# Moving the v products, transposes and mean squares of an mLSTM head within a hand-ordered schedule

## The reference

```python
p = jnp.exp(dmat - m_t[..., None]) * jnp.einsum('bhtd,bhsd->bhts', qc, kc)
num = w_inter[..., None] * jnp.einsum('bhtd,bhdv->bhtv', qc, C) + jnp.einsum('bhts,bhsv->bhtv', p, vc)
den = w_inter * jnp.einsum('bhtd,bhd->bht', qc, n) + jnp.sum(p, axis=-1)
h_c = num / jnp.maximum(jnp.abs(den), jnp.exp(-m_t))[..., None]
...
hs = rms_norm(hs) * h_norm.astype(f32).reshape(H, dv)
out = jax.nn.sigmoid(o.astype(f32)) * hs.reshape(B, S, H * dv)
return out.astype(h.dtype) @ w_out
```

## The kernel before

| half e | PE, after its 12 matmuls | ACT, after `w_hi` | DVE, after `w_lo` | POOL |
|---|---|---|---|---|
| 6 + 5h | scores(h), L1784 | | | |
| 7 + 5h | | exp(h) into `weights`, L870 | | mask(h), L587 |
| 8 + 5h | | | probs(h), L1241 | |
| 10 + 5h | products with v (h), L1766 to L1768 | | | |
| 11 + 5h | | squares, L878 and L881 | | |
| 12 + 5h | | tanh into `o_sig`, L862 | mean squares h_ms(h), L1250 | pow, L595; sigmoid, L597; then mask(h+1) |
| 13 + 5h | | | gated(h), L1260 | |
| 14 + 5h | transposes of gated(h), L1755 | | | |
| 15 + 5h | | o_hi(h), L888 | o_lo(h), L1274 | |

## Time and profile before

### The profile page before, as it was taken

One profiled execution on the slowest core, in us unless ns is written; L12 is line 12 of the kernel. 1 busy time (PEld: TensorE's weight loads), 2 busy tenths in 40 slices (PEclk: granted clock), 3 DMA queues, 4 the chain that ended last, 5 costly groups with the idle time before them and its releaser, 6 DMA issues.

```text
span 1179.1 us, 17187 instructions
## 1 busy us (share of the span) xinstructions
PE 1160.9 (98%) x5926; PEld 989.2 (84%) x5926; DVE 922.5 (78%) x1006; ACT 632.1 (54%) x920; POOL 165.2 (14%) x168
## 2 busy tenths in 40 slices
PE   5999999999999999999999999999999999999998
PEld 5888888888888888888888888888888888888887
DVE  6899997998889979888886547888885456777667
ACT  4444565666653556655554445555554455555442
POOL 1000140101221220221220001221220001221200
PEclk9999999999999999999999999999999999999999
DMA  9999999999999976987876577788775666666552
GB/s 367 397 401 402 400 355 341 360 406 372 337 362 362 400 206 179 266 232 231 246 235 215 194 231 223 210 260 235 213 249 180 206 185 185 197 188 179 202 176 86
DMA packets 260603, 314.57 MB, mean 267 GB/s; under 512 B 6241, under 2 KB 187177, under 8 KB 251849
## 3 DMA queue, kind: packets, MB, share of 16 engines
q1 hardware_dynamic: 259488, 312.50, 79.5%
q0 software_dynamic: 592, 1.22, 0.4%
q10 hardware_dynamic: 474, 0.21, 0.1%
HBM read 311.80 MB, written 2.11 MB: 266 GB/s over the span
## 4 chain that ended last, share of the span: by engine, by line
PE 73%; DMA 12%; DVE 8%; issue 3%; POOL 2%; ACT 1%; SPq 0%; DVEq 0%; ACTq 0%
PE ps L1484 27%; PE ps L1490 14%; PE ps L1524 9%; PE ps L1526 9%; PE ps L1525 9%; DMA m<-in_l_w_mod_dram 6%; DVE acc L1112 3%; DMA mod_raw<-in_l_w_mod_dram 3%; DMA raw<-in_l_w_in_dram 2%; DVE w_lo L1093 2%; POOL small L595 1%; PE ps L1593 1%; PE ps L1594 1%; DMA x<-in_x_dram 1%; PE ps L1652 1%
## 5 line engine op out<-in xcount | busy, mean ns | idle before, releaser
L662 ACT ACTIVATE w_hi<-raw 128x1024 fp32r<-128x1024 f32 x384 | 406.0, 1058 | 347.3 <-PE ps L1526 156.0
L1093 DVE TENSOR_TENSOR w_lo<-raw,w_hi 128x1024 fp32r<-128x1024 f32 x384 | 471.3, 1230 | 151.8 <-ACT w_hi L662 150.5
L1484 PE MATMUL ps<-hm,w_hi 128*128 128x512 f32 x1406 | 338.8, 391 | 0.2 <-DVE hm L1381 0.2
L1484 PEld LDWEIGHTS ps<-hm,w_hi 128*128 128x128 f32 x1406 | 257.2, 188 | 49.2 <-DVE hm L1381 0.4
L1490 PEld LDWEIGHTS ps<-hm,w_lo 128*128 128x128 f32 x1408 | 182.7, 191 | 8.2
L1490 PE MATMUL ps<-hm,w_lo 128*128 128x256 f32 x1408 | 185.2, 283 | 0.0
L1593 PE MATMUL ps<-w_hi,hm 128*128 128x512 f32 x380 | 150.8, 397 | 0.0
L1594 PE MATMUL ps<-w_lo,hm 128*128 128x512 f32 x380 | 148.0, 390 | 0.0
L1596 PE MATMUL ps<-w_hi,hm 128*128 128x512 f32 x352 | 137.2, 390 | 0.0
L1526 PE MATMUL ps<-w_hi,act_lo 128*128 128x512 f32 x344 | 133.8, 389 | 0.0
L1525 PE MATMUL ps<-w_lo,act_hi 128*128 128x512 f32 x344 | 133.8, 389 | 0.0
(11 more groups left out here) (204 smaller groups left out, 1140.4 us busy)
## 6 DMA issues: line engine op xcount, KB each, us to landing
raw<-in_l_w_up_dram SPq DMA_DIRECT2D x88, 1024.0 KB, 5.8
raw<-in_l_w_in_dram SPq DMA_DIRECT2D x96, 512.0 KB, 12.1
mod_raw<-in_l_w_mod_dram SPq DMA_DIRECT2D x48, 1024.0 KB, 7.5
raw<-in_l_w_down_dram SPq DMA_DIRECT2D x44, 1024.0 KB, 5.0
m<-in_l_w_mod_dram SPq DMA_DIRECT2D x32, 640.0 KB, 14.2
raw<-in_l_w_out_dram SPq DMA_DIRECT2D x16, 1024.0 KB, 8.8
m<-in_l_w_mod_dram SPq DMA_DIRECT2D x15, 768.0 KB, 12.7
mod_third<-in_l_w_mod_dram SPq DMA_DIRECT2D x8, 1024.0 KB, 7.9
```

Source lines behind the costliest of these rows:

```text
L662: nc.scalar.activation(w_hi[:, v % 4, :], raw_half(v), ACT.Copy).then_inc(w_hi_made, 1)
L1093: nc.vector.tensor_tensor(w_lo[:, v % 4, :], raw_half(v), w_hi[:, v % 4, :].bitcast(f32), ALU.subtract)\
L1484: return mm(ps[:, 4 + w % 4, :], w_hi[:, v % 4, j * P:(j + 1) * P], both, start=(k == 0), stop=stop, skip_group_check=True)
```

## The change

E_PV goes from 10 to 11 and E_HT from 14 to 15; E_SCORES stays. All that hangs on these two offsets moves by one half: on PE the products with v of head h now stand in half 11 + 5h, the half of the next head's scores, and directly ahead of them in the order of `attend`; the transposes go to half 15 + 5h. On ACT the squares go to half 12 + 5h (behind the next head's exponentials), tanh to 13 + 5h, o_hi to 16 + 5h. On DVE the mean squares go to 13 + 5h, gated to 14 + 5h, o_lo to 16 + 5h. Half 13 + 5h is also that of the next head's probs, and in DVE's `attend` the block of the mean squares is moved ahead of the block of probs. POOL's order is not touched. No instruction is added or removed.

```diff
@@ -88,7 +88,7 @@
-    E_SCORES, E_PV, E_HT, E_HEAD = 6, 10, 14, 5
+    E_SCORES, E_PV, E_HT, E_HEAD = 6, 11, 15, 5
     E_GATE = 19
@@ -1233,14 +1233,6 @@
             def attend(e):
 
-                h = head_at(e, E_SCORES + 2)
-                if h is not None:
-                    dve.wait_ge(masked, h + 1)
-                    dve.wait_ge(scores_made, h + 1)
-                    wait_from_1(dve, pv_done, h)
-                    nc.vector.scalar_tensor_tensor(out=probs[:], in0=ps[:, 1, 0:SEQ + P],
-                                                   scalar=float(DK) ** -0.5, in1=weights[:],
-                                                   op0=ALU.mult, op1=ALU.mult).then_inc(probs_made, 1)
                 h = head_at(e, E_PV + 2)
                 if h is not None:
                     dve.wait_ge(den_sq_made, h + 1)
@@ -1251,6 +1243,14 @@
                                                        scalar=a_em[:, 2 + t, h:h + 1],
                                                        in1=h_ss[:, t:t + 1], op0=ALU.max, op1=ALU.add)\
                                  .then_inc(h_ms_made, 1)
+                h = head_at(e, E_SCORES + 2)
+                if h is not None:
+                    dve.wait_ge(masked, h + 1)
+                    dve.wait_ge(scores_made, h + 1)
+                    wait_from_1(dve, pv_done, h)
+                    nc.vector.scalar_tensor_tensor(out=probs[:], in0=ps[:, 1, 0:SEQ + P],
+                                                   scalar=float(DK) ** -0.5, in1=weights[:],
+                                                   op0=ALU.mult, op1=ALU.mult).then_inc(probs_made, 1)
```

## The result

The changed kernel takes 1186.87 us (median of 6, 1185.95 to 1187.57), the kernel before, run beside it, 1181.61 (median of 6, 1177.57 to 1181.84). The ratio is 1.0059, 95% interval 1.0047 to 1.0072: slower by about 0.6%. The forecast was 1187.0. Run again beside other executions of the kernel before (e9), the changed kernel gave 1185.90 and 1.0045 [1.0028, 1.0061]. The profiled execution has a span of 1185.1 us, against 1179.1 before, and a granted clock of 0.999.

The account below looks back on a forecast made before the run. DVE's queue, with its waits for the mask, was taken to pace the heads; after the change, a 17.97 us loop would. +5.7 us by half 41 and -0.4 in head 6 give +5.3 on 1181.7: 1187.0 us, range 1183.0 to 1193.2.

Parts of the forecast that it names:

- The pow: POOL's pow in heads 0 to 6 shortens from 1.60 to 0.72 us; rival that it stays 1.60, chance 0.15.
- Mean squares to probs: On DVE, from start to start, 2.14 us instead of 3.02, with `w_lo` (1.14 us) now paid in full ahead.
- The loop: Through all engines, transposes of one head to the next: 17.97 us, 17.37 without g_lo, setting the pitch.
- The wait for `w_hi`: DVE newly waits about 0.6 us per head for ACT's `w_hi`, because the loop exceeds DVE's own 17.14 us.
- the rival of DVE's queue alone: The loop doesn't bind; DVE's queue sets a pitch of 17.14 us: +1.8 us, 1183.5 us, chance 0.13.
- PE's wait for gated: In the heads, PE waits for gated about 1 us per head instead of 0.5; transposes 18.0 us apart.
- DVE is unmoved up to the `w_lo` of half 12: Starting point of the sum, at 249.06 us on DVE, from which head 0's transposes come at 258.28.
- my signs of being wrong: Gated less than 2.7 us later in head 0, or a wait for DMA data at `w_hi` or `add_mod`.
- The end of the stage: Head 5's transposes at 347.53, +5.7 us at half 41's scores, -0.4 us in head 6, in all +5.3 us.
- From span to time: 2.6 us between span and median, taking the forecast span of 1184.4 us to a time of 1187.0 us.
- The rival "faster": Gated leaves the POOL chain and PE's 3.9 us of waiting for it go: 1177.8 us, chance 0.07.

Follow-up runs that it names:

- e9: The changed kernel run again, unaltered, beside other executions of the kernel before: 1185.90 us, ratio 1.0045.
- e3: The changed kernel with two DVE products of 128 x 512, both inputs in SBUF, added behind the mean squares: 1192.93 us, ratio 1.0108.
- e4: The changed kernel with two DVE products of 128 x 512, one input in PSUM, added behind the mean squares: 1185.67 us, ratio 1.0053.
- e2: The changed kernel with only the mean squares put back ahead of the `w_lo` of their half: 1179.71 us, ratio 0.9997.
- e1: The changed kernel with gated moved ahead of the `w_lo` that stands before it, DVE's work unchanged: 1182.03 us, ratio 1.0017.
- e8: The kernel before with transposes one half later and POOL's mask of the next head ahead of pow: 1178.69 us, ratio 0.9990.
- e10: The kernel before run again, unaltered, as if it were a change, with a second profile: 1181.04 us, ratio 1.0001.
- e6: The kernel before with POOL making the mask of the next head ahead of the pow: 1178.59 us, ratio 0.9989.
- e5: The changed kernel with POOL making the mask of the next head ahead of the pow: 1178.85 us, ratio 0.9988.
- e7: The kernel before with only gated and transposes one half later (`E_HT` from 14 to 15): 1179.13 us, ratio 0.9996.
- e11: The kernel before with the `add_mod` of half 11 cut from 2048 to 256 columns, so DVE reaches head 0 early: 1178.60 us, ratio 0.9990.

## Why the prediction was right

1. *The pow.* Forecast 0.72 us (0.70 from start to start), measured 0.69 to 0.72 in heads 0 to 6. The cause, DVE's instructions with two SBUF inputs, is shown by e3 beside e4.
2. *Mean squares to probs.* 2.14 forecast, 2.11 measured. DVE pays the `w_lo` in full in front of it. e2 shows that this is the part of the change that costs.
3. *The loop.* 17.97 us with the g_lo, 17.37 without: measured 295.00 - 277.09 = 17.91 and 17.35 (348.20 - 330.85). The terms hold one by one: transposes to products with v 3.24 (3.26 forecast), on to the scores 1.30 (1.32), on to `w_hi` 3.62 (3.61), on to `w_lo` 1.09 (1.10). The wait for `w_hi`, forecast at 0.6 us, is 0.59 to 0.62 in heads 1 to 5; the rest of the 5.8 us are two longer waits behind, 1.54 and 1.24. (The forecast's own terms give 17.85 - 17.14 = 0.7 for it.) e1 tells it from the rival of DVE's queue alone, 17.14, which is what e1 itself came to.
4. *PE's wait for gated.* Forecast "about 1 us per head", listed 0.69 to 0.70 in heads 1 to 4 and 1.08 in head 5. Start to start PE loses 0.92 in heads 1 to 4: from the gate sums to the transposes are 4.14 us (272.95 to 277.09), and 3.22 in e8 (271.08 to 274.30), where PE doesn't wait. Another 0.39 a head goes at the gate sums themselves, which the forecast didn't have. I had said 18.0 between transposes, which is the period with the g_lo; the mean is 17.80.
5. *Head 0, 0.9 us too early.* The step "DVE is unmoved up to the `w_lo` of half 12" failed. The `add_mod` before it came later than before (246.79 there):

```profile
247.67 2.35 DVE L1112 SCALAR_TENSOR_TENSOR acc<-mod_raw,cT,acc 128x2048 f32<-128x2048 f32 x1 [1.36 <-issue]
```

What it waited for, the profile doesn't show. In this execution its 0.88 us make the error: the `w_lo` of half 13 follows that of half 12 without a wait. But without this delay head 0 would not have been on time either: in e9 the `add_mod` came at 246.47 and the transposes of head 0 still started at 259.09, because there the `w_lo` of half 13 waited (timeline of DVE):

```profile
250.99 1.23 DVE L1093 TENSOR_TENSOR w_lo<-raw,w_hi 128x1024 fp32r<-128x1024 f32 x1 [1.03 <-ACT w_hi L662]
```

So head 0 can hang on `w_hi` like the others. I had counted DVE's instructions from 249.06 on and asked for `w_hi` only from half 18. Of my signs of being wrong, one did show in the profile: ACT's `w_hi` at 248.98 waited 1.35 us for DMA data, and such waits came to 8.4 us in 6 between 230 and 385 us, against 4.9 in 3 before. It didn't make the result: e10, the kernel before, has 9.5 us in 6 of them, and e9 has none at that place and the same head 0 within 0.1 us.
6. *The end of the stage.* Head 5: 347.53 forecast, 348.20 measured; the late start of head 0 is in it, and the periods between were a little shorter than summed. At the scores of half 41 the changed kernel is 352.76 - 346.39 = 6.4 us late, where I had 5.7. From head 6 on PE has no wait for gated, as forecast; this gives back 0.3 us of the 0.4 that I had. In all +6.0 us where I had +5.3.
7. *From span to time.* I took 2.6 us between the profiled span, 1179.1, and the median, 1181.7. An execution has 1.8 us outside its span (1186.91 - 1185.1, and 1181.67 - 1179.9 in e10). The other 0.8 was that the profiled execution of the kernel before was a little faster than its median. This error of -0.8 us and the +0.7 of point 6 cancelled: the 0.1 us between forecast and median is luck, the mechanism is not.
8. *The rival "faster", 1177.8.* Its condition was right (it needs a shorter path than the change gives), its price was too high. In e6, where PE doesn't wait for gated, heads 0 to 7 take 369.82 - 255.06 = 114.8 us, against 371.93 - 254.68 = 117.3 before, so 2.5 us were to be had and not 3.9. Neither row of waits gives this number. Of the 3.9 us, 3.5 were PEld's, weight loads that wait while PE still computes, which is too much; the 0.4 of PE itself are far too little, because most of PE's loss isn't listed. The last matmul and the transposes of head 2, before:

```profile
287.67 0.39 PE L1596 MATMUL ps<-w_hi,hm 128*128 128x512 f32 x1
288.06 0.66 PE L1755 MATMUL ps<-ident,gated 128*128 128x128 f32 x4
```

and in e6:

```profile
287.48 0.39 PE L1596 MATMUL ps<-w_hi,hm 128*128 128x512 f32 x1
287.70 0.60 PE L1755 MATMUL ps<-ident,gated 128*128 128x128 f32 x4
```

The start comes 0.39 us after the last one instead of 0.22, and no wait stands beside it, since the modelled 0.39 us of the matmul reach up to it. So what I said of the profile, that such waits are listed apart, holds only for what exceeds this overlap. In the changed kernel the rows miss about as much; that is why their difference, +5.8 us, still comes near the loss of 6.0.
9. *Not foreseen:* the two rhythms of the kernel before. The profiles put 2.1 us between them up to head 5, more than a third of what the change costs, and the profile of one execution doesn't show it. That the unchanged kernel changes between them from execution to execution is inferred from the times.

## What to carry to other kernels

Before an operation is moved behind another, look whether that other one lies inside a wait: what is hidden there is paid for once it stands in front of it, here 1.14 us a head against the 0.9 us that the shorter wait gave back, and the loop that it closed cost more than this difference. Price a move by the longest loop that closes through all engines, from one head to the same point of the next, and not by the fullest queue; start that sum one item ahead of the first one that you think is touched. And price what PE loses from start to start, against a stretch in which it doesn't wait: the rows of waits gave 0.4 us for PE and 3.5 more for its weight loads, and the loss was 2.5.

## What the runs showed of the hardware

- The length of a small POOL operation is set by what DVE runs beside it: the pow of 128 x 2 takes 0.69 to 0.72 us alone, 1.60 to 1.77 beside one `w_lo` or two products from SBUF, and 3.87 beside an `add_mod` with a `w_lo` right behind it. In this last case it lasts across both. Beside products with a PSUM input it stays at 0.69 (e4).
- It holds for POOL's other operations: the sigmoid of 128 x 512 takes 0.61, 1.14 or 3.54 us, the mask of 128 x 256 takes 0.40 or 3.65 (e2, e5). DVE can lose as well: the `add_mod` took 2.70 instead of 2.35 us four times in e5 between head 1 and head 4, and 3.38 in the kernel before at 392.40, where it starts inside two POOL additions of 128 x 512 (390.11 to 393.64).
- Who comes first matters: in e2, pow started 0.26 us ahead of the `w_lo` and took 0.69 us; in e7, it started 0.03 us behind one (250.75 and 250.72) and took 1.77. By this the kernel before can go through the heads in two rhythms, 16.88 or 16.47 us a head. In e11 a head start of 1.6 us at the first mean squares gave the short one; how little would do, no run shows.
- TensorE's granted clock fell to its lower level (0.50) for some 3 us in the profiled e3, from about 261 us on, behind a wait of 2.62 us that ended at 259.75; in the changed kernel, behind a wait of 2.31 us at the same place, it stayed at 1.00.
